# Two more columns in the first of the three products of every input chunk

## The chip, the cores and the metric

The kernel runs on one core of a Trainium2 chip, in one launch. The metric is the device time of that core in microseconds. TensorE is called PE in the profile, its weight loads PEld, VectorE DVE, ScalarE ACT, GpSimd POOL; SyncE (SP) issues the weight stream's DMAs.

## What is computed

The reference is two transformer blocks in float32 over one sequence of 256 tokens with 1024 features. The first holds SwiGLU FFNs, an even mixer (banded and stick-breaking attention), an odd mixer (dilated attention) and two cross attentions; the second holds FFNs and two mixers of differential attention beside a chunked mLSTM. Of its time nearly all goes into dense products of this kind:

```
def swiglu_ffn(x, w_gu, w_down):
    gate, up = jnp.split(x @ w_gu, 2, axis=-1)
    return (jax.nn.silu(gate) * up) @ w_down
```

The sequence is short, so every weight is used once, for 256 tokens.

## The kernel before

Activations are kept feature-major: 8 chunks of 128 features by T = 256 tokens. A float32 product is made out of three float32r products. Each operand is split into a high part (hi, rounded to float32r) and the remainder (lo), and hi by hi, hi by lo and lo by hi are summed in PSUM. The input's two parts lie next to each other per chunk, in `a_two` and `b_two`, [P, C, 2, T]; `a_hi`, `a_lo`, `b_hi`, `b_lo` are views of them.

The weights come as a stream of 829 tiles of 128 x 1024 float32, in the order of use. SP loads each into one of RAW = 4 buffers (`raw`), ACT casts it to `w_hi` (L1072), DVE takes the remainder to `w_lo` (L1508), both rings of RING = 6. PE waits for both parts of a tile (`wait_split`) before its first product.

All matmuls go through the helper `mm` (L462). There are these uses of a weight tile on PE:

- `w_tile` (L468): one output tile of 128 features by 256 tokens, 8 chunks of three products with the weights standing in the array and the tokens moving. It fills columns 0 to 255 of a PSUM bank of 512. FFN gate and up tiles go through it, and so do the projections of the mixers (through `w_next`).
- `three` (L490), `first_three` (L610 in `ffn`) and `tail_part` (L966): the same three products per chunk, but with three tiles taken chunk by chunk as the input comes ready, or a tile in parts.
- `down` in `ffn`: one input chunk into all 8 output chunks, which are two to a bank (`acc(c)`), so both halves of those banks are in use.
- `v_half` (L529): the weights move and the activations stand; two blocks of 128 tokens share a bank, both halves in use.

There are 14 stages in a fixed order, 8 of them FFNs (`STAGES`). An FFN has 22 gate/up pairs and 22 down tiles; after the first few, a `Fori` of 9 turns does two pairs and two down tiles a turn. In it PE runs gate, up and then the down tile of two pairs before. DVE and ACT read the gate and up banks (`gate_up_of`, two pairs of banks in turn), and make the product that `down` needs.

The order of PE's work is the order in which the code above is written. PE waits on semaphores for the weight split, for its banks to be read, and for its inputs.

Of the kernel before, what the change touches and what calls it, by code (L numbers as in the profile page):

```python
# [25 lines left out]
ALU = mybir.AluOpType  # L26
# [5 lines left out]
T = 256  # L32
C = D // P
# [6 lines left out]
RAW = 4  # L40
RING = 6
AHEAD = 4
FFN_TILES = 3 * FJ
C_PATTERNS = ((128, 1), (512, 4), (2048, 16))

# [98 lines left out]
def build(nc, stream_d, x_d, mem_d, vec_d, con_d, biasa_d, biasc_d, heads_d, out_d, stages=STAGES):  # L144
    total = sum(TILES[s] for s, _ in stages)
    with ExitStack() as ctx:
# [8 lines left out]
        a_two = sb("a", [P, C, 2, T], F32R)  # L155
# [46 lines left out]

        def gate_up_of(j, after_mixer):

            return bank[4 + 2 * (j % 2)][:, 0:T], bank[2 if j == 0 and after_mixer else 5 + 2 * (j % 2)][:, 0:T]

        ones = con[:, CON["ones"]:CON["ones"] + P]
        halves = con[:, CON["halves"]:CON["halves"] + 32]
# [236 lines left out]
        def _(pe):  # L445
            t = Tally()
# [10 lines left out]
            act_of = {"a": (a_hi, a_lo), "b": (b_hi, b_lo)}  # L457
            fresh = {}
            rescaled = [False]

            def mm(out, lhsT, rhs, start, stop, shared=False):
                return nc.tensor.matmul(out, lhsT, rhs, start=start, stop=stop, skip_group_check=shared)  # L462
# [5 lines left out]
            def w_tile(n, slot, out, hi, lo, ready=None):  # L468

                wait_split(n)  # L470
                for c in range(C):
                    if ready:
                        ready(c)
                    wh, wl = w_hi[:, slot, c * P:(c + 1) * P], w_lo[:, slot, c * P:(c + 1) * P]
                    mm(out, wh, hi[:, c, :], c == 0, False)
                    mm(out, wh, lo[:, c, :], False, False)
                    last = mm(out, wl, hi[:, c, :], False, c == C - 1)
                return last.then_inc(tile_mm, 1)

            def w_bank(read_by, count):  # L480
# [9 lines left out]
            def three(buf, tiles, where):  # L490

                k, n = turn[0] % 2, at[0]
                outs = [bank[i] for i in where or (W_BANKS[k], W_BANKS[1 - k], T_BANK)]
                hi, lo = act_of[buf]
                ready = fresh.pop(buf)
                for i in range(3):
                    wait_split(n + i)
                    evac_of[tiles[i]] = t.next(w_evac)
                if where is None:
                    turn[0] += 2  # L500
                    last_read[k], last_read[1 - k] = (w_evac, evac_of[tiles[0]]), (w_evac, evac_of[tiles[1]])
                for c in range(C):
                    ready(c)
                    for i in range(3):
                        slot = (n + i) % RING
                        wh, wl = w_hi[:, slot, c * P:(c + 1) * P], w_lo[:, slot, c * P:(c + 1) * P]
                        mm(outs[i][:, 0:T], wh, hi[:, c, :], c == 0, False)
                        mm(outs[i][:, 0:T], wh, lo[:, c, :], False, False)
                        last = mm(outs[i][:, 0:T], wl, hi[:, c, :], False, c == C - 1)
                        if c == C - 1:  # L510
                            last.then_inc(tile_mm, 1)
                at[0] += 3

            def w_next(buf, read_by, where=None):
                if where is None:
                    out = w_bank(read_by, 1)
                else:
                    out = bank[where]
                    t.next(read_by)
                w_tile(at[0], at[0] % RING, out[:, 0:T], *act_of[buf], fresh.pop(buf, None))  # L520
                at[0] += 1

            def v_half(buf, half):
# [81 lines left out]
            def ffn(k, after_mixer):  # L605
                base = k * FJ
                n0 = at[0]
                ready = each(norm_lo)

                def first_three():  # L610

                    outs = [*gate_up_of(0, after_mixer), gate_up_of(1, after_mixer)[0]]
                    for i in range(3):
                        wait_split(n0 + i)
                    for c in range(C):
                        ready(c)
                        for i in range(3):
                            slot = (n0 + i) % RING
                            wh, wl = w_hi[:, slot, c * P:(c + 1) * P], w_lo[:, slot, c * P:(c + 1) * P]
                            mm(outs[i], wh, hi[:, c, :], c == 0, False, True)  # L620
                            mm(outs[i], wh, lo[:, c, :], False, False, True)
                            last = mm(outs[i], wl, hi[:, c, :], False, c == C - 1, True)
                            if c == C - 1:
                                last.then_inc(tile_mm, 1)

                def gate_up(n, slot, j, J):
                    for part, freed in ((0, gate_read), (1, up_read)):
                        pe.wait_ge(freed, J - 1)
                        w_tile(n + part, (slot + part) % RING, gate_up_of(j, False)[part], hi, lo)

                def down(n, slot, jj, J, first=False, final=False):


                    wait_split(n)
                    pe.wait_ge(hlo_done, J + 1)
                    for c in range(C):
                        out = acc(c)
                        wh, wl = w_hi[:, slot, c * P:(c + 1) * P], w_lo[:, slot, c * P:(c + 1) * P]
                        mm(out, wh, h[0][:, jj, :], first and c % 2 == 0, False, True)
                        mm(out, wh, h[1][:, jj, :], False, False, True)  # L640
                        last = mm(out, wl, h[0][:, jj, :], False, final, True)
                        if final and c % 2 and c < C - 1:
                            last.then_inc(acc_done, 1)
                    last.then_inc(tile_mm, 1)

                (hi, lo), h = act_of["a"], act_of["b"]
                s0 = n0 % RING
                first_three()
                if not rescaled[0]:
                    sum_squares(FFN_STAT)  # L650
                w_tile(n0 + 3, (s0 + 3) % RING, gate_up_of(1, False)[1], hi, lo, sums_at_half(FFN_STAT))
                gate_up(n0 + 4, (s0 + 4) % RING, 2, base + 2)
                pe.wait_ge(root_ready, t.so_far(root_ready))
                down(n0 + 6, s0, 0, base, first=True)
                gate_up(n0 + 7, (s0 + 1) % RING, 3, base + 3)
                down(n0 + 9, (s0 + 3) % RING, 1, base + 1)
                with pe.Fori(0, (FJ - 4) // 2) as i:
                    for u in range(2):
                        n, slot, J = i * 6 + (n0 + 10 + 3 * u), (s0 + 10 + 3 * u) % RING, i * 2 + (base + 4 + u)
                        gate_up(n, slot, 4 + u, J)  # L660
                        down(n + 2, (slot + 2) % RING, u, J - 2)
                for j in (FJ - 2, FJ - 1):
                    n = n0 + FFN_TILES - FJ + j
                    down(n, n % RING, j % 2, base + j, final=j == FJ - 1)
                at[0] += FFN_TILES
                if k >= 4:
                    keep_going(1)
                    sum_of_parts()
                    keep_going(7 if k < 7 else 0)
                t.next(x_ready, C)  # L670
# [294 lines left out]
            def tail_part(tile, hi, lo, c0, c1):  # L965
# [6 lines left out]
                out, slot = tail_out[tile]  # L972
                for c in range(c0, c1):
                    wh, wl = w_hi[:, slot, c * P:(c + 1) * P], w_lo[:, slot, c * P:(c + 1) * P]
                    mm(out[:, 0:T], wh, hi[:, c, :], c == 0, False)
                    mm(out[:, 0:T], wh, lo[:, c, :], False, False)
                    last = mm(out[:, 0:T], wl, hi[:, c, :], False, c == C - 1)
                if c1 == C:
# [511 lines left out]
        def _(dve):  # L1490
# [144 lines left out]
            def ffn(k, following, after_mixer):  # L1635
# [2 lines left out]

                def gate_scale(j, n):
                    dve.wait_ge(tile_mm, n + 1)  # L1640
                    nc.vector.tensor_tensor(sil[:, j % 2, :], gate_up_of(j, after_mixer)[0], r, ALU.mult)\  # L1641
                        .then_inc(gate_read, 1)

                def up_scale(j, n):
                    dve.wait_ge(tile_mm, n + 1)
                    nc.vector.tensor_tensor(hmid[:, j % 2, :], gate_up_of(j, after_mixer)[1], r, ALU.mult)\  # L1646
                        .then_inc(up_read, 1)

                def raw_copy(out, source, n, signal):
# [27 lines left out]
                    h_low(u, J)  # L1677

                split_to(n0 + 5)
                raw_copy(sil[:, 0, :], gate_up_of(0, after_mixer)[0], n0, gate_read)  # L1680
                raw_copy(hmid[:, 0, :], gate_up_of(0, after_mixer)[1], n0 + 1, up_read)
                raw_copy(sil[:, 1, :], gate_up_of(1, after_mixer)[0], n0 + 2, gate_read)
                if rescaled[0]:
                    split_to(n0 + 6)
                factors(r, True)
# [690 lines left out]
```

## Time and profile before

| | us |
|---|---|
| median of 3 runs | 2601.88 |
| lowest and highest | 2599.9, 2601.97 |
| span of the profiled execution | 2597.9 |
| PE busy in it | 2562.5 |
| DVE busy | 1787.7 |
| ACT busy | 1389.7 |

The profiled execution is known by its span, from first to last instruction; the median lies 4.0 us above it. PE is busy nearly always, but products are pipelined: one takes some 276 ns from start to end, and the next starts after less than half of that. Its rate is read from starts, or from how many products start in a window, not from its busy share.

### The profile page before, as it was taken

The numbers are of one execution on the slowest core, as the hardware profiler recorded it, in microseconds if no ns is written. First come the engines' busy times: TensorE is split into PE (matmuls) and PEld (weight loads), VectorE is DVE, ScalarE is ACT, GpSimd is POOL, SyncE is SP. The second block draws the span as 40 slices with busy tenths as digits, with TensorE's granted clock in tenths as the row PEclk, the third lists the DMA queues.
The fourth block names the chain that finished last, engine by engine and source line by source line (L and its number), as shares of the span: only waits on it lengthen the run. The fifth ranks groups of instructions, "written<-read, shape, count | busy, mean of one in ns | idle before, by whom it ended". The sixth has DMA issues, their size and how long they took to land.

```text
span 2597.9 us, 56642 instructions
## 1 busy us (share of the span) xinstructions
PE 2562.5 (99%) x21484; PEld 2481.9 (96%) x21484; DVE 1787.7 (69%) x2852; ACT 1389.7 (53%) x2228; POOL 190.8 (7%) x265
## 2 busy tenths in 40 slices
PE   8999999999999999999999999999999999999998
PEld 8998899999998899999999998999999999989998
DVE  7667586667667586767667657776676686677765
ACT  5456556445445755545445555654454465555543
POOL 1001001000000201000000260000000005300000
PEclk9999999999999999999999999999999999999999
DMA  7654245665554354665664543555555545335563
GB/s 272 210 194 138 85 143 181 226 208 188 193 192 158 104 166 142 202 191 176 208 194 158 182 148 105 167 167 193 191 166 188 186 158 173 130 114 179 178 193 114
DMA packets 122830, 445.87 MB, mean 172 GB/s; under 512 B 13688, under 2 KB 14712, under 8 KB 122688
## 3 DMA queue, kind: packets, MB, share of 16 engines
q1 hardware_dynamic: 120816, 436.79, 51.4%
q0 software_dynamic: 1872, 7.11, 0.8%
q8 instruction: 99, 1.62, 0.3%
q14 instruction: 43, 0.35, 0.0%
HBM read 442.79 MB, written 1.05 MB: 171 GB/s over the span
## 4 chain that ended last, share of the span: by engine, by line
PE 93%; DVE 4%; ACT 1%; DMA 1%; issue 0%; SPq 0%; POOL 0%; DVEq 0%; ACTq 0%; POOLq 0%
PE bank L462 92%; DVE w_lo L1508 1%; PE bank L830 1%; DVE x L1623 1%; DVE z L1619 1%; DVE a L1535 0%; DVE score L1559 0%; DVE rstd_x L1527 0%; DMA x<-in_x_dram 0%; DMA heads<-in_heads_dram 0%; ACT score L1304 0%; ACT w_hi L1072 0%; ACT a L1093 0%; DVE rt L1806 0%; DVE rstd_m L1574 0%
## 5 line engine op out<-in xcount | busy, mean ns | idle before, releaser
L462 PE MATMUL bank<-a,w_hi 128*128 128x256 f32 x7472 | 1304.5, 279 | 4.5 <-DVE a L1535 2.7
L1508 DVE TENSOR_TENSOR w_lo<-raw,w_hi 128x1024 fp32r<-128x1024 f32 x829 | 1012.2, 1225 | 201.6 <-ACT w_hi L1072 199.8
L462 PEld LDWEIGHTS bank<-a,w_hi 128*128 128x128 f32 x7472 | 1132.0, 188 | 18.5 <-issue 12.9
L462 PE MATMUL bank<-a,w_lo 128*128 128x256 f32 x3736 | 1035.6, 277 | 0.0
L1072 ACT CAST w_hi<-raw 128x1024 fp32r<-128x1024 f32 x829 | 842.7, 1044 | 51.9 <-DMA raw<-in_stream_dram 48.7
L462 PE MATMUL bank<-b,w_hi 128*128 128x256 f32 x4800 | 839.5, 278 | 2.8 <-DVE w_lo L1508 2.8
L462 PEld LDWEIGHTS bank<-b,w_hi 128*128 128x128 f32 x4800 | 727.4, 188 | 10.6 <-issue 5.7
L462 PEld LDWEIGHTS bank<-a,w_lo 128*128 128x128 f32 x3736 | 702.7, 188 | 0.0
L462 PE MATMUL bank<-b,w_lo 128*128 128x256 f32 x2400 | 664.8, 277 | 0.0
L462 PEld LDWEIGHTS bank<-b,w_lo 128*128 128x128 f32 x2400 | 450.9, 188 | 0.0
L1132 ACT CAST b<-hmid 128x256 fp32r<-128x256 f32 x132 | 53.7, 407 | 393.9 <-PE bank L462 383.5
L1646 DVE TENSOR_TENSOR hmid<-bank,rstd_x 128x256 f32<-128x256 f32 x168 | 71.2, 424 | 161.3 <-PE bank L462 161.2
L1128 ACT ACTIVATE sil<-sil 128x256 f32<-128x256 f32 x176 | 73.5, 418 | 149.9 <-DVE sil L1641 142.9
L1508 DVE TENSOR_TENSOR b<-hmid,b 128x256 fp32r<-128x256 f32 x132 | 56.1, 425 | 126.9 <-ACT b L1132 126.6
L462 PE MATMUL bank<-w_hi,a 128*128 128x256 f32 x736 | 130.7, 281 | 0.0
L2185 POOL TENSOR_SCALAR score<-score,rr 128x128 f32<-128x128 f32 (+1 forms) x96 | 44.5, 479 | 1100.9 <-DVE rr L1874 804.2
L462 PEld LDWEIGHTS bank<-w_hi,a 128*128 128x128 f32 x736 | 111.9, 188 | 3.4 <-issue 2.5
L1745 DVE TENSOR_TENSOR z<-bank,rstd_x 128x256 f32<-128x256 f32 x121 | 51.1, 422 | 77.2 <-PE bank L462 76.4
L462 PE MATMUL bank<-w_lo,a 128*128 128x256 f32 x368 | 102.2, 278 | 0.0
L1132 ACT CAST a<-hmid 128x256 fp32r<-128x256 f32 x44 | 17.9, 407 | 136.0 <-PE bank L462 132.7
L1660 DVE TENSOR_TENSOR hmid<-sil,hmid 128x256 f32<-128x256 f32 x176 | 74.8, 425 | 6.8 <-ACT sil L1128 1.1
L1641 DVE TENSOR_TENSOR sil<-bank,rstd_x 128x256 f32<-128x256 f32 x160 | 67.8, 424 | 13.0 <-PE bank L462 2.8
(191 smaller groups left out, 1924.3 us busy)
## 6 DMA issues: line engine op xcount, KB each, us to landing
raw<-in_stream_dram SPq DMA_DIRECT2D x829, 512.0 KB, 3.7
z<-in_biasc_dram POOLq DMA_DIRECT2D x6, 512.0 KB, 4.6
z<-in_biasa_dram POOLq DMA_DIRECT2D x3, 512.0 KB, 5.0
x<-in_x_dram SPq DMA_DIRECT2D x2, 512.0 KB, 8.1
v<-in_mem_dram POOLq DMA_DIRECT2D x2, 512.0 KB, 5.7
out_dram<-x SPq DMA_DIRECT2D x8, 128.0 KB, 1.9
con<-in_con_dram POOLq DMA_DIRECT2D x1, 848.0 KB, 6.4
vec<-in_vec_dram POOLq DMA_DIRECT2D x1, 417.0 KB, 5.6
```

The source lines that it names most:

```text
L462: return nc.tensor.matmul(out, lhsT, rhs, start=start, stop=stop, skip_group_check=shared)
L830: last = nc.tensor.transpose(out[:, col:col + P], p[:, src:src + P], ident)
L1072: nc.scalar.copy(w_hi[:, slot, :], raw[:, raw_slot, :]).then_inc(hi_split, 1)
L1128: nc.scalar.activation(sil[:, jj, :], sil[:, jj, :], ACT.Silu).then_inc(silu_done, 1)
L1132: nc.scalar.copy(high_of["b"][:, jj, :], hmid[:, jj, :]).then_inc(hhi_done, 1)
L1508: return nc.vector.tensor_tensor(out, a, hi.bitcast(F32), ALU.subtract)
L1619: nc.vector.tensor_tensor(temp[:, c, :], x[:, c, :], rt[:, 0, 0:T], ALU.mult).then_inc(dve_step, 1)
L1641: nc.vector.tensor_tensor(sil[:, j % 2, :], gate_up_of(j, after_mixer)[0], r, ALU.mult)\
L1646: nc.vector.tensor_tensor(hmid[:, j % 2, :], gate_up_of(j, after_mixer)[1], r, ALU.mult)\
L1660: nc.vector.tensor_tensor(hmid[:, jj, :], sil[:, jj, :], hmid[:, jj, :], ALU.mult)\
L1745: nc.vector.tensor_tensor(z[:, tile, :], out[:, 0:T], rstd[norm][:, :], ALU.mult).then_inc(w_evac, 1)
L2185: last = nc.gpsimd.tensor_scalar(p, p, rr[:, k, b:b + 1], 1.0, ALU.mult, ALU.mult)
```

## The change

A function `first_product` takes the place of the first `mm` (hi by hi) in `w_tile`, `three`, `first_three` and `tail_part`. It reads T + EXTRA = 258 columns in place of 256 and writes 258 columns of the bank. The two more columns read are the first two of the same chunk's lo part, which lies right behind hi (`both_of`); they land in columns 256 and 257 of the bank, in the half that these tiles leave unused. The other two products of the chunk stay at 256 columns. `down` and `v_half` are not changed. The readers of the banks take columns 0 to 255 as before; `gate_up_of` now gives whole banks, and its readers slice them.

```
+EXTRA = 2
...
-            return bank[4 + 2 * (j % 2)][:, 0:T], bank[2 if j == 0 and after_mixer else 5 + 2 * (j % 2)][:, 0:T]
+            return bank[4 + 2 * (j % 2)], bank[2 if j == 0 and after_mixer else 5 + 2 * (j % 2)]
...
+            both_of = dict((id(hi), two[:, :, :, :].rearrange("p c h t -> p c (h t)")) for hi, two in ((a_hi, a_two), (b_hi, b_two)))
+
+            def first_product(out, wh, hi, c, shared=False):
+
+                n = T + EXTRA
+                mm(out[:, 0:n], wh, both_of[id(hi)][:, c, 0:n], c == 0, False, shared)
...
-                    mm(out, wh, hi[:, c, :], c == 0, False)
-                    mm(out, wh, lo[:, c, :], False, False)
-                    last = mm(out, wl, hi[:, c, :], False, c == C - 1)
+                    first_product(out, wh, hi, c)
+                    mm(out[:, 0:T], wh, lo[:, c, :], False, False)
+                    last = mm(out[:, 0:T], wl, hi[:, c, :], False, c == C - 1)
```

The same three lines change in `three`, `first_three` and `tail_part`. No instruction moves on any engine. On PE, in the FFN loop, this is the end of an up tile (input `a`), the step to the next weight tile, and the beginning of a down tile (input `b`). Before:

```order
L462 MATMUL bank<-a,w_hi 128x256 x2
L462 MATMUL bank<-a,w_lo 128x256
L465 REGISTER_ALU
L462 MATMUL bank<-b,w_hi 128x256 x2
L462 MATMUL bank<-b,w_lo 128x256
```

And with the change, at the same place:

```order
L469 MATMUL bank<-a,w_hi 128x258
L469 MATMUL bank<-a,w_hi 128x256
L469 MATMUL bank<-a,w_lo 128x256
L472 REGISTER_ALU
L469 MATMUL bank<-b,w_hi 128x256 x2
L469 MATMUL bank<-b,w_lo 128x256
```

The first of the two w_hi products of an up tile's chunk has 258 columns; those of the down tile are as they were.

## Rows read from the trace of the kernel before

**Rows 1.** The page: span, and part 1, busy time, share of the span, instructions

```profile
span 2597.9 us, 56642 instructions
...
PE 2562.5 (99%) x21484; PEld 2481.9 (96%) x21484; DVE 1787.7 (69%) x2852; ACT 1389.7 (53%) x2228; POOL 190.8 (7%) x265
```

**Rows 2.** The page's part 4, the chain that ended last, by line

```profile
PE bank L462 92%; DVE w_lo L1508 1%; PE bank L830 1%; DVE x L1623 1%; DVE z L1619 1%; DVE a L1535 0%; DVE score L1559 0%; DVE rstd_x L1527 0%; DMA x<-in_x_dram 0%; DMA heads<-in_heads_dram 0%; ACT score L1304 0%; ACT w_hi L1072 0%; ACT a L1093 0%; DVE rt L1806 0%; DVE rstd_m L1574 0%
```

**Rows 3.** The view of waits, PE: who waited for whom, us, times, longest

```profile
PE bank L462 <- ACT w_hi L1072: 5.2, 1, 5.2
```

**Rows 4.** Groups of PE, shapes apart: w_lo products, standing weights | busy, mean ns

```profile
L462 PE MATMUL bank<-a,w_lo 128*128 128x256 f32 x3736 | 1035.6, 277 | 0.0
...
L462 PE MATMUL bank<-b,w_lo 128*128 128x256 f32 x2400 | 664.8, 277 | 0.0
```

**Rows 5.** The chain in order of time, 1728 to 2090 us: start, us, what

```profile
1728.58 163.89 PE bank L462 x1442
...
1915.88 170.27 PE bank L462 x1442
```

**Rows 6.** Windows, L462 on PE: length, busy us (x products), clock, DMA share, GB/s

```profile
1732.00:1892.00 160.00, 160.00 (x1414) 1.00 0.62 203
1920.00:2080.00 160.00, 160.00 (x1361) 1.00 0.60 195
```

**Rows 7.** The timeline of PE, a fast stretch, then a slow one: start, us

```profile
1820.14 0.39 PE L462 MATMUL bank<-b,w_hi 128*128 128x256 f32 x2
1820.37 0.28 PE L462 MATMUL bank<-b,w_lo 128*128 128x256 f32 x1
1820.48 0.39 PE L462 MATMUL bank<-b,w_hi 128*128 128x256 f32 x2
...
2010.30 0.40 PE L462 MATMUL bank<-b,w_hi 128*128 128x256 f32 x2
...
2010.65 0.40 PE L462 MATMUL bank<-b,w_hi 128*128 128x256 f32 x2
```

**Rows 8.** The timeline of PE, the start of the same two stages

```profile
1728.58 0.48 PE L462 MATMUL bank<-b,w_hi 128*128 128x256 f32 x2 [1.01 <-DVE w_lo L1508]
...
1729.02 0.39 PE L462 MATMUL bank<-b,w_hi 128*128 128x256 f32 x2
1729.25 0.28 PE L462 MATMUL bank<-b,w_lo 128*128 128x256 f32 x1
...
1915.88 0.47 PE L462 MATMUL bank<-b,w_hi 128*128 128x256 f32 x2 [0.76 <-DVE w_lo L1508]
...
1916.31 0.40 PE L462 MATMUL bank<-b,w_hi 128*128 128x256 f32 x2
1916.55 0.28 PE L462 MATMUL bank<-b,w_lo 128*128 128x256 f32 x1
```

**Rows 9.** The timeline of PEld, weight loads, in the fast and the slow stretch

```profile
1820.37 0.30 PEld L462 LDWEIGHTS bank<-b,w_hi 128*128 128x128 f32 x2
...
2010.18 0.31 PEld L462 LDWEIGHTS bank<-b,w_hi 128*128 128x128 f32 x2
```

**Rows 10.** L830's products: timeline, and the line's own, min/median/max ns

```profile
1539.87 0.49 PE L830 MATMUL bank<-con,score 128*128 128x128 f32 x3
...
L830 PE MATMUL bank<-con,score x152: 270/273/330, 238.2 to 2244.2; 128*128 128x128 f32 x152
```

**Rows 11.** Windows as in rows 6: the first and the last slow stretch

```profile
192.50:200.50 8.00, 8.00 (x70) 1.00 0.20 61
...
2409.00:2413.00 4.00, 4.00 (x36) 1.00 0.01 4
```

**Rows 12.** Windows as in rows 6: weights moving, a slow and a fast stretch

```profile
1500.00:1515.00 15.00, 15.00 (x130) 1.00 0.53 173
...
2142.00:2162.00 20.00, 20.00 (x179) 1.00 0.63 208
```

**Rows 13.** The page's part 5: DVE's half of the weight split | busy, mean ns

```profile
L1508 DVE TENSOR_TENSOR w_lo<-raw,w_hi 128x1024 fp32r<-128x1024 f32 x829 | 1012.2, 1225 | 201.6 <-ACT w_hi L1072 199.8
```

More of the change, by code:

```diff
@@ L506, in three @@
                         wh, wl = w_hi[:, slot, c * P:(c + 1) * P], w_lo[:, slot, c * P:(c + 1) * P]
-                        mm(outs[i][:, 0:T], wh, hi[:, c, :], c == 0, False)
+                        first_product(outs[i], wh, hi, c)
                         mm(outs[i][:, 0:T], wh, lo[:, c, :], False, False)
@@ L519, in w_next @@
                     t.next(read_by)
-                w_tile(at[0], at[0] % RING, out[:, 0:T], *act_of[buf], fresh.pop(buf, None))
+                w_tile(at[0], at[0] % RING, out, *act_of[buf], fresh.pop(buf, None))
                 at[0] += 1
@@ L619, in first_three @@
                             wh, wl = w_hi[:, slot, c * P:(c + 1) * P], w_lo[:, slot, c * P:(c + 1) * P]
-                            mm(outs[i], wh, hi[:, c, :], c == 0, False, True)
-                            mm(outs[i], wh, lo[:, c, :], False, False, True)
-                            last = mm(outs[i], wl, hi[:, c, :], False, c == C - 1, True)
+                            first_product(outs[i], wh, hi, c, True)
+                            mm(outs[i][:, 0:T], wh, lo[:, c, :], False, False, True)
+                            last = mm(outs[i][:, 0:T], wl, hi[:, c, :], False, c == C - 1, True)
                             if c == C - 1:
@@ L974, in tail_part @@
                     wh, wl = w_hi[:, slot, c * P:(c + 1) * P], w_lo[:, slot, c * P:(c + 1) * P]
-                    mm(out[:, 0:T], wh, hi[:, c, :], c == 0, False)
+                    first_product(out, wh, hi, c)
                     mm(out[:, 0:T], wh, lo[:, c, :], False, False)
@@ L1640, in gate_scale @@
                     dve.wait_ge(tile_mm, n + 1)
[L1641 removed]
+                    nc.vector.tensor_tensor(sil[:, j % 2, :], gate_up_of(j, after_mixer)[0][:, 0:T], r, ALU.mult)\
                         .then_inc(gate_read, 1)
@@ L1645, in up_scale @@
                     dve.wait_ge(tile_mm, n + 1)
-                    nc.vector.tensor_tensor(hmid[:, j % 2, :], gate_up_of(j, after_mixer)[1], r, ALU.mult)\
+                    nc.vector.tensor_tensor(hmid[:, j % 2, :], gate_up_of(j, after_mixer)[1][:, 0:T], r, ALU.mult)\
                         .then_inc(up_read, 1)
@@ L1679, in ffn @@
                 split_to(n0 + 5)
-                raw_copy(sil[:, 0, :], gate_up_of(0, after_mixer)[0], n0, gate_read)
-                raw_copy(hmid[:, 0, :], gate_up_of(0, after_mixer)[1], n0 + 1, up_read)
-                raw_copy(sil[:, 1, :], gate_up_of(1, after_mixer)[0], n0 + 2, gate_read)
+                raw_copy(sil[:, 0, :], gate_up_of(0, after_mixer)[0][:, 0:T], n0, gate_read)
+                raw_copy(hmid[:, 0, :], gate_up_of(0, after_mixer)[1][:, 0:T], n0 + 1, up_read)
+                raw_copy(sil[:, 1, :], gate_up_of(1, after_mixer)[0][:, 0:T], n0 + 2, gate_read)
                 if rescaled[0]:
```

## The prediction

> **What bounds the kernel now.** I read first the page's busy times, then the chain that ended last, then the PE groups, and last the starts of single products. PE is busy for 99% of the span [rows 1], and matmuls of the helper line L462 alone hold 92% of the chain [rows 2]. PE's waits are small: the longest entry is 5.2 us, once, for the first weight split [rows 3]. TensorE's granted clock reads full, 1.00, in every stretch used below, which is its upper level of 2.4 GHz. So the time is a count of products times their spacing, and whatever changes the spacing changes the end one for one.
>
> The count: where the weights stand in the array, a chunk takes three products (w_hi by the input's high part, w_hi by its low part, w_lo by its high part). The w_lo ones are 3736 + 2400 = 6136 [rows 4], so there are 6136 such triples, 18,408 products. The triples of the FFN's down products, which the change leaves alone, are 22 tiles x 8 chunks x 8 FFN stages = 1408. The change touches the other 4728.
>
> The spacing is not one number. The chain holds the steady part of two FFN stages in a row, the same 1442 products each: 163.89 us in the one, 170.27 us in the other, 6.38 us apart [rows 5]. The windows say the same: 1414 products start in 160 us of the first stage and 1361 in 160 us of the second, which is 113.2 ns and 117.6 ns each at the same clock, and DMA share is no higher in the slow one (0.60 against 0.62) [rows 6]. The single starts show it as a rhythm: in the fast stretch one triple follows the other by 0.34 us (1820.14, 1820.48), in the slow one by 0.35 (2010.30, 2010.65) [rows 7]. By the starts over a whole stretch I take 113.3 and 117.8 ns, 4.4 ns apart (6.38 us / 1442 gives the same).
>
> Which rhythm a stretch has is settled within the first three or so products after PE has stood still, and then kept: from the first product to the fourth the two stages take 0.44 and 0.43 us, from the fourth to the sixth 0.23 and 0.24 us, and they stay apart for 1442 products [rows 8]. Nothing waits in between. So the slow rhythm is not work of its own; it is a state that PE's own streams fall into.
>
> **What the change does, part by part.**
>
> 1. *Two more columns in 4728 products.* TensorE takes 256 columns at 2.4 GHz in 106.7 ns, and 258 in 107.5, so 0.83 ns more each: 4728 x 0.83 = 3.9 us if all of it lay in the spacing. I take 0 for it. In the fast rhythm a product starts every 113.3 ns, which leaves 6.6 ns behind its last column, and the next weight load begins only as a product begins (1820.37 in both views), the next product 0.11 us after that (1820.48) [rows 7, 9]: the load, not the stream of columns, seems to release the next product. The nearest rows of another kind are 128-column fp32 products of L830, each with its own load: three of them take 0.49 us with 0.273 us for one, so some 0.11 us each [rows 10]. They stay at or under the fast spacing. The bounds for this part are therefore 0 and +3.9 us in the fast rhythm; a product that is pushed past some further slot is rival C.
>
> The row shows 113.3 ns. The Trainium skill (TensorE: Matmul & The Clock Gate, Back-to-back issue gap) puts the warm gap of one product at its columns over 2.4 GHz plus 2.5 ns, which would be 109.2 ns before and 110.0 after, and by that rule the change costs 3.9 us if the stream sets the spacing. The same page (LDWEIGHTS) puts a weight load at its columns over 1.2 GHz, 106.7 ns for 128, untouched here, so if the load sets the spacing the columns are free. No trace row gives 109.2 for these products, so neither rule describes the spacing whole.
>
> 2. *What becomes of the slow rhythm.* This is the term of the sum. With weights standing, I find 26 stretches of nine or more slow gaps, 3288 products in all: the first at 192.4 us with 70, the last at 2408.8 us with 37, the longest the FFN stage at 1916 us with 1438; three others have 226 and one 261 [rows 6, 11]. They cost 3288 x 4.44 ns = 14.6 us. A rhythm that repeats exactly triple after triple (353.3 ns, against 340.0) needs the three products to be alike. With the change each triple has one product whose columns end 0.83 ns later, in a rhythm whose own excess is only 4.4 ns a product, so the point at which the streams meet moves with each triple. I expect that the slow rhythm is not held by such triples and runs on until it falls into the fast one, which has the slack of part 1. The bounds: nothing gained (0), and all of it (-14.6 us). I take nearly all, -14 us, with some 0.5 us for the 26 settlings.
>
> 3. *What is not touched.* The down products keep three alike, but they come 24 at a time behind 48 changed ones, and a rhythm once found is kept. The products in which the weights move (v halves, 1488) are not changed; 934 of them are slow in 23 stretches, as in the window at 1500 us with 130 in 15 us where another of the same kind has 179 in 20 us [rows 12]. They cost 4.1 us; I leave that as it is, since they start behind short waits of their own. DVE, ACT, POOL and the DMA issues have the same instructions. The slices of the bank they read are the same 256 columns; the two extra columns land where nobody reads. The faster PE asks for weights no sooner than it does in the other stages, where DVE's half of the split (1225 ns a tile) [rows 13] fits in a tile of 24 x 113.3 = 2720 ns. So nothing new comes late.
>
> The sum, against the profiled execution: span 2597.9 - 14 = 2584; the median of the three runs is 4.0 us above that span, so 2601.9 - 14 = 2588 us.
>
> **Rivals.**
>
> A. The forecast: the slow rhythm goes with weights standing. 2587 if all goes, 2598 if only the shorter stretches do, since the FFN stage at 1916 us holds 6.4 of the 14.6 us. Chance 0.42. For: two rhythms, one program, chosen at a restart. Against: I infer from starts how the streams meet; no row shows it.
>
> B. Nothing to measure: the weight load sets the spacing in both rhythms and hides the columns in both, or they cost up to their 3.9 us. 2598 to 2606. Chance 0.22. For: the load begins with the product before it in both rhythms, and its row reads 0.30 and 0.31 us for two [rows 9].
>
> C. Slower, and the one on the other side: the fast rhythm is the delicate one. If the first product's 258 columns end past the point at which the next product or its load takes its turn, the next must wait for another turn. The price is what the slow rhythm shows, since there is no other: 353.3 - 340.0 = 13.3 ns for a triple at full price, half of it (6.7 ns) if the other two products catch up. Over 4728 triples that is 31 us at half, so 2633; at full price for all triples that are fast now, (18,408 - 3288) / 3 = 5040, 67 us, 2669. It decides at 113.3 ns: if a product's natural time is within 0.83 ns of it, C holds. The L830 rows stand against, with 0.11 us. Chance 0.19.
>
> D. The choice is drawn afresh: both rhythms survive, but the first products after each restart fall otherwise. One of eight FFN stages is slow now, while of all stretches with a rhythm of their own (a dozen gaps or more) 49 in 151 are, by the starts. A draw at that rate would give two or three slow stages, 6.4 us each: 2608 to 2615. Chance 0.17 (of which 0.02 for a lucky draw that comes out faster).
>
> **How the numbers follow.** Likeliest is A, 2588 us. A's own range is 2580 to 2598. A range for 8 in 10 takes in A, B, D and the lower half of C: 2579 to 2636. About 0.2% (5 us) is what a measurement of this kernel can tell from no change, so faster is A and the lucky part of D, 0.44; same is B and a little of D, 0.22; slower is C and the rest of D, 0.34.
>
> **What the profile of the changed kernel would show.** Part 1: in a steady FFN stage 1414 products in 160 us as now; 1400 or fewer would say that the columns are in the spacing. Part 2: the steady part of every FFN stage at 164 us for 1442 products in the chain, the one at 1916 us too; if one still reads 170, the slow rhythm is held by uneven triples and A is wrong. Part 3: the windows of v halves as now, some slow. C would show as triples of 0.35 us in nearly every stage, D as other stages slow than now. The prediction fails if the two rhythms turn on something that I can't see in these rows, such as where operands lie in SBUF, which the change leaves alone.

## The result and the profile after

| | before | after |
|---|---|---|
| median, us | 2601.88 | 2674.23 |
| runs | 3, 2599.9 to 2601.97 | 3, 2673.84 to 2677.43 |
| span of the profiled execution, us | 2597.9 | 2671.9 |

The changed kernel is slower: 1.0288 of the time before, 95% interval 1.0255 to 1.032. The forecast was 2588 us, range 2579 to 2636.

The page after, span and part 1, to read beside [rows 1]:

```profile
span 2671.9 us, 56642 instructions
...
PE 2639.9 (99%) x21484; PEld 2559.4 (96%) x21484; DVE 1789.2 (67%) x2852; ACT 1388.6 (52%) x2228; POOL 189.1 (7%) x265
```

The products are as many as before, 21484, and PE is busy for the same share. DVE and ACT have not changed. The time is again in the spacing of the products. From the chain in order of time of the changed kernel, the steady part of the same two FFN stages as in [rows 5], and above them the longest piece:

```profile
412.64 443.45 PE bank L469 x3728
...
1780.89 170.05 PE bank L469 x1442
...
1974.34 170.06 PE bank L469 x1442
```

And the longest piece in the kernel before:

```profile
403.69 428.23 PE bank L462 x3728
```

The two stages, 163.89 and 170.27 us before, now take 170.05 and 170.06: the fast one has lost 6.2 us, the slow one has gained 0.2. The longest piece has gone from 428.23 to 443.45 us for the same 3728 products. Windows inside the two stages, as in [rows 6] (length, busy us, products, clock, DMA share, GB/s):

```profile
1783.00:1943.00 160.00, 160.00 (x1361) 1.00 0.59 195
1977.00:2137.00 160.00, 160.00 (x1360) 1.00 0.59 195
```

1361 and 1360 products in 160 us, where the fast stage had 1414, with the clock at 1.00. Taken alone, this reads as if the slow rhythm (353.3 ns for the three products of a chunk, a triple) were everywhere. The timeline says otherwise. Five starts from the changed kernel, the end of a down tile (256 columns throughout) and the start of a gate tile:

```profile
1850.94 0.39 PE L469 MATMUL bank<-b,w_hi 128*128 128x256 f32 x2
...
1851.29 0.39 PE L469 MATMUL bank<-b,w_hi 128*128 128x256 f32 x2
...
1851.62 0.40 PE L469 MATMUL bank<-a,w_hi 128*128 128x258 f32 x2
...
1851.98 0.40 PE L469 MATMUL bank<-a,w_hi 128*128 128x258 f32 x2
...
1852.34 0.40 PE L469 MATMUL bank<-a,w_hi 128*128 128x258 f32 x2
```

The down triple takes 1851.29 - 1850.94 = 0.35 us here at 10 ns a step (340 to 341 ns by the starts), so the down tiles run in the fast rhythm. The triples with a 258-column product take 0.36 us, 1851.62 to 1851.98 to 1852.34. By all starts in the trace, counting every triple that another follows within 400 ns, 4054 of 4475 changed triples take 359 to 361 ns (mean of all 359.6), and 1219 of 1400 down triples take 339 to 341. The means of other runs below are taken in the same way. So there is a third rhythm, of 360 ns a triple, that the profile before did not show: slower than the slow one's 353.3. Within a changed triple the products follow at 118.9, 118.4 and 122.3 ns on average, so all three are late and not just the one behind the long product.

The sum of it: both traces have the same 21484 products in the same order, so each spacing can be set against its own from before. Where it is under 150 ns in both, those of the changed triples have grown by 76.5 us in all (13,979 spacings), those of the v halves by 2.0, and those of the down tiles have shrunk by 1.3. That is 77 us; the spans are 74.0 apart, so the longer spacings, with the waits in them, have given some 3 us back.

### The profile page after: what moved, and what is told of

It is laid out like the page before. It is cut to its first block, busy times and chain, and to the rows that moved or that the text cites. A ratio compares the mean times of both kernels' runs of the same rounds, so it can differ in the third digit from the quotient of the medians.

```text
span 2671.9 us, 56642 instructions
## 1 busy us (share of the span) xinstructions
PE 2639.9 (99%) x21484; PEld 2559.4 (96%) x21484; DVE 1789.2 (67%) x2852; ACT 1388.6 (52%) x2228; POOL 189.1 (7%) x265
## 4 chain that ended last, share of the span: by engine, by line
PE 94%; DVE 4%; ACT 1%; issue 0%; DMA 0%; SPq 0%; DVEq 0%; ACTq 0%
PE bank L469 93%; DVE w_lo L1515 1%; PE bank L837 1%; DVE x L1630 1%; DVE z L1626 1%; DVE a L1542 0%; DVE score L1566 0%; DVE rstd_x L1534 0%; DMA raw<-in_stream_dram 0%; ACT a L1100 0%; ACT w_hi L1079 0%; DVE rt L1813 0%; DVE rstd_m L1581 0%; ACT score L1311 0%; DVE z L1611 0%
## 5 line engine op out<-in xcount | busy, mean ns | idle before, releaser
L469 PE MATMUL bank<-a,w_hi 128*128 128x256 f32 (+1 forms) x7472 | 1357.5, 283 | 3.0 <-DVE a L1542 2.2
L469 PEld LDWEIGHTS bank<-a,w_hi 128*128 128x128 f32 x7472 | 1157.2, 188 | 16.8 <-issue 12.4
L469 PE MATMUL bank<-a,w_lo 128*128 128x256 f32 x3736 | 1061.5, 284 | 0.0
L469 PE MATMUL bank<-b,w_hi 128*128 128x258 f32 (+1 forms) x4800 | 859.5, 281 | 1.7 <-DVE w_lo L1515 1.7
L469 PEld LDWEIGHTS bank<-b,w_hi 128*128 128x128 f32 x4800 | 737.4, 188 | 9.5 <-issue 4.6
L469 PEld LDWEIGHTS bank<-a,w_lo 128*128 128x128 f32 x3736 | 710.5, 190 | 0.0
L469 PE MATMUL bank<-b,w_lo 128*128 128x256 f32 x2400 | 674.6, 281 | 0.0
```

## The experiments

All runs but those of the inputs' place are written from the changed kernel, and times are compared with the kernel before on the same chip, whose medians in the four sets were 2604.6, 2602.9, 2605.3 and 2603.1 us.

### Shorter, longer by 16 columns, and a pair that makes up for itself

A shorter product, with the first back at 256 columns:

```
-EXTRA = 2
+EXTRA = 0
...
-                    mm(out[:, 0:T], wh, lo[:, c, :], False, False)
+                    mm(out[:, 0:T - 2], wh, lo[:, c, 0:T - 2], False, False)
```

> The first product of every chunk is back at 256 columns; the second one (hi by lo) has 254, so the last two tokens miss that small term. Measured so far: a changed triple takes 360 ns in place of 340 or 353. Theory 1 (alignment: the fast rhythm of 113.3 ns needs products whose lengths are all alike or keep step with a clock of the chip; any odd length, longer or shorter, throws the next product off step): the triples stay near 355 to 360 ns though they do less work, 2655 to 2680 us. Theory 2 (length: only a product that is too long misses its turn, and 258 columns is too long): a shorter product costs nothing, 2580 to 2605 us.

Measured: 2650.9 us, ratio 1.0183 (1.0139 to 1.0226). Changed triples take 353.1 ns on average, though each has less work than before. It's not the two columns of work that cost, and not only that a product is too long for its turn: a product two columns too short costs 46 us, where one two columns too long costs 70 to 72.

The FFN stages of this run are not all alike:

```profile
1764.43 168.04 PE bank L469 x1442
...
2467.48 170.27 PE bank L469 x1442
```

In the one at 1764 us the changed triples take 344 to 357 ns and most down triples 340. The one at 2467 us is in the slow rhythm throughout: all 304 triples with a 254-column product that were counted take 352 to 355 ns. So uneven triples can hold the slow rhythm.

Sixteen more columns:

```
-EXTRA = 2
+EXTRA = 16
```

> EXTRA = 16: the first product of every chunk has 272 columns, 14 more than in the changed kernel, or 6.7 ns more work in each of 4728 products. Theory 1 (alignment): start times in the trace of before keep to a step of 6.67 ns, which is 16 columns at 2.4 GHz, so 272 columns stay in step: a triple takes 340 + 6.7 = 347 ns at most, 2601.9 + 31 = 2633 us or less (2619 if the slow stretches go too), faster than with 258 columns. Theory 2 (length): longer is worse, 360 ns or more a triple, 2674 us or more.

Measured: 2675.9 us, ratio 1.0279 (1.0235 to 1.0323), 358.7 ns a triple. Theory 1 in the form in which I had it, that any multiple of 16 columns stays in step, is wrong. The product behind the 272-column one comes 124.3 ns later and the next two at 117.5 and 116.8: near the slow rhythm's spacing, with 6.7 ns more for the 16 columns behind the long one.

The first product two longer, the second two shorter:

```
-                    mm(out[:, 0:T], wh, lo[:, c, :], False, False)
+                    mm(out[:, 0:T - 2], wh, lo[:, c, 0:T - 2], False, False)
```

> First product 258 columns, second 254 (the last two tokens miss the hi by lo term), third 256: the sum of a triple is again 768. Theory 1 (alignment): two products in the triple start off step, but the third is back on it, so the triple should cost less than 360 ns, some 345 to 355, 2620 to 2655 us. Theory 2 (length of the long product alone): as the changed kernel, 2670 to 2676 us.

Measured: 2630.0 us, ratio 1.0099 (1.0069 to 1.013), most triples 346 or 347 ns. Two odd products that cancel cost less than either alone. So the number of odd products is not what counts. That the products have to come back to a step fits this run, but 272 columns, 16 more, did not behave so.

### All three alike

```
+            def second_product(out, wh, hi, c, shared=False):
+                n = T + (EXTRA if c < C - 1 else 0)
+                mm(out[:, 0:n], wh, flat_of[id(hi)][:, (2 * c + 1) * T:(2 * c + 1) * T + n], False, False, shared)
...
-                    last = mm(out[:, 0:T], wl, hi[:, c, :], False, c == C - 1)
+                    last = third_product(out, wl, hi, c)
```

The second product reads on into the next chunk's high part, the third into its own chunk's low part.

> 258 columns in all three products of a chunk in the tiles that go through w_tile with all their input ready (the FFN's gate and up tiles and most of the mixers'; the last chunk's second product stays at 256, and the other uses have 258 in the first and third). The prediction held that a rhythm needs three products that are alike. If likeness is what counts, these triples take 340 to 343 ns, 2600 to 2635 us. If the length itself has to fit (256 columns do, 258 don't), they take 353 ns or more, 2650 to 2690 us.

Measured: 2716.3 us, ratio 1.043 (1.0397 to 1.0463). A triple of three 258-column products takes 365.5 ns on average, 121.8 ns a product, and the single ones are spread from 360 to 374, with no length that most of them have. So three like products need not give a rhythm that repeats, and they are slower here than the changed kernel's uneven ones. The down tiles, fast behind the changed kernel's triples, are slow behind these (353.4 ns).

The same with EXTRA = 16:

> 272 columns in all three products where all input is ready (elsewhere in the first and third), as the run with 258 columns in all three. If the fast rhythm needs alike products in step with 16 columns, these triples take 340 + 20 = 360 ns, about as long as the changed kernel's 360, 2670 to 2690 us. If 272 columns have only the slow rhythm, 117.8 + 6.7 = 124.4 ns a product and 373 ns a triple, some 2730 us or more.

Measured: 2738.0 us in one run; three 272-column products take 370.6 ns, 123.5 each, near the 124.4 of the slow rhythm with 6.7 ns more. For 272 columns no fast rhythm shows: none of these triples takes less than 369 ns, where 340 + 20 = 360 would be the fast one.

### What sets the pace: fewer and more columns

Half of the second product left out, 128 columns in place of 256:

```
-EXTRA = 2
+EXTRA = 0
...
-                    mm(out[:, 0:T], wh, lo[:, c, :], False, False)
+                    mm(out[:, 0:128], wh, lo[:, c, 0:128], False, False)
```

> Leaves half of the hi by lo product out: first and third product of a chunk have 256 columns, the second has 128, in the same 4728 chunks. The second's columns take 53 ns, half of a weight load's 128 columns would still have to come. Theory 1 (the load sets the fast spacing of 113.3 ns, as the prediction had it): the product after the short one still comes some 110 to 118 ns later, a changed triple takes 340 to 360 ns, 2590 to 2680 us. Theory 2 (the stream of columns sets it): it comes well under 100 ns later, a triple takes 290 to 300 ns, some 2370 to 2420 us.

Measured: 2630.4 us in one run. Most changed triples take 343 to 350 ns, none less than 341, with half of the second product's columns gone. The starts of the products (a row with x2 has the first and second):

```profile
1799.98 0.34 PE L469 MATMUL bank<-a,w_hi 128*128 128x256 f32 x2
1800.15 0.33 PE L469 MATMUL bank<-a,w_lo 128*128 128x256 f32 x1
1800.32 0.34 PE L469 MATMUL bank<-a,w_hi 128*128 128x256 f32 x2
```

And of the weight loads in the same triples:

```profile
1800.10 0.19 PEld L469 LDWEIGHTS bank<-a,w_lo 128*128 128x128 f32 x1
1800.21 0.30 PEld L469 LDWEIGHTS bank<-a,w_hi 128*128 128x128 f32 x2
1800.44 0.19 PEld L469 LDWEIGHTS bank<-a,w_lo 128*128 128x128 f32 x1
```

The product behind the short one starts early, 0.17 us after the first (1799.98 to 1800.15), and the next one waits, another 0.17. The loads show why. They begin at 1800.10 and 1800.21 (a pair of w_hi), and the next of w_lo at 1800.44: three steps, 0.34 us from w_lo to w_lo. They go on at a little over 0.11 us each, though the products have a sixth less to stream. So the columns don't set the floor, and it is not a fixed distance from product to product either, since the one behind the short product starts 60 ns after it. What is left, and goes once with each product, is the load of the weights, as the prediction had it; that is by exclusion, for no run changed the loads.

All three products at 240 columns (chunk 0's first product stays at 256):

```
-EXTRA = 2
+EXTRA = -16
...
-                n = T + EXTRA
+                n = T + (EXTRA if c else 0)
...
-                    mm(out[:, 0:T], wh, lo[:, c, :], False, False)
-                    last = mm(out[:, 0:T], wl, hi[:, c, :], False, c == C - 1)
+                    mm(out[:, 0:240], wh, lo[:, c, 0:240], False, False)
+                    last = mm(out[:, 0:240], wl, hi[:, c, 0:240], False, c == C - 1)
```

> All three products of a chunk have 240 columns (the last 16 tokens get only the first chunk's first product; 16 columns are 6.7 ns, the step on which start times lie). Theory 1 (load sets the fast spacing): 340 ns a triple at best, as before, 2590 to 2680 us. Theory 2 (stream sets it, and the fast rhythm holds for lengths that are a multiple of 16 columns): 320 ns a triple, 2602 - 4728 x 20 ns = 2507 us. Theory 3 (stream sets it, but 240 columns have only the slow rhythm, 117.8 - 6.7 = 111.1 ns a product): 333 ns, some 2570 us.

Measured: 2601.3 us in one run. The timeline:

```profile
1800.24 0.39 PE L469 MATMUL bank<-a,w_hi 128*128 128x240 f32 x2
1800.46 0.28 PE L469 MATMUL bank<-a,w_lo 128*128 128x240 f32 x1
1800.58 0.39 PE L469 MATMUL bank<-a,w_hi 128*128 128x240 f32 x2
```

0.34 us a triple, about as the fast rhythm with 256 columns, with 16 columns fewer in each product. By all starts the mean is 338.6 ns, where columns alone would have taken 20 ns off; the shortest take 332, so 340 is not quite the floor. (The down tiles, left at 256, are slow in this run, 353 ns, so the time is not below the kernel before.) The Trainium skill (TensorE: Matmul & The Clock Gate, LDWEIGHTS) has a load's time go by its own columns, 106.7 ns for 128, whatever the product streams; that is 6.6 ns under the 113.3 measured between products, and no run here changed a load's columns.

512 columns in the first product:

```
-EXTRA = 2
+EXTRA = 256
```

> EXTRA = 256: the first product has 512 columns, so the stream of columns and not the weight load must set its spacing. With 272 columns the product after the long one came 124.3 ns later, 6.5 ns more than the slow rhythm's 117.8, which is the time of 16 columns. If off the fast rhythm the columns' stream sets the spacing, this one comes 117.8 + 106.7 = 224.5 ns later, a changed triple takes some 460 ns and the kernel some 3150 us. If a weight load set it, the first product would hide part of its added columns, 213 to 218 ns, 3110 us or less.

Measured: 3181.1 us in one run. The product behind the 512-column one comes 230.0 ns later on average (226 to 233), nearer to 224.5 than to 218: with long products the stream of columns sets the spacing, with 17 ns on top of its 213.3.

So the runs fit two chains: loads at 111 to 113 ns each, and the stream of columns, 106.7 ns for 256 of them and something on top that depends on how they meet. At 256 columns the two are nearly equal. That the rhythms come from this is argued, and not shown.

### What the fast rhythm keeps step with

The kernel before, all products at 256 columns, with the inputs a and b moved in SBUF by 8 bytes:

```
-        sb("gap_b", [P, 64])
-        b_two = sb("b", [P, C, 2, T], F32R)
+        sb("gap_b", [P, 56])
+        b_two = sb("b", [P, C * 2 * T + 8], F32R)[:, 2:2 + C * 2 * T].rearrange("p (c h t) -> p c h t", c=C, h=2)
```

and the same for `a_two`; everything else stays where it was.

> The kernel before with the input arrays a and b moved by 8 bytes (2 columns) in SBUF, all products at 256 columns. Open is what the fast rhythm keeps step with. If it is where a product's columns begin or end in SBUF (258 columns end 8 bytes further), the fast rhythm is lost in all products with a or b moving, whose triples take 353 ns or more: 2665 us or more. If it is the count of columns alone, nothing changes: 2592 to 2616 us as before.

Measured: 2703.4 us, ratio 1.0391 (1.0343 to 1.044). The timeline of an FFN stage:

```profile
1850.42 0.40 PE L462 MATMUL bank<-b,w_hi 128*128 128x256 f32 x2
...
1850.78 0.40 PE L462 MATMUL bank<-b,w_hi 128*128 128x256 f32 x2
```

0.36 us a triple, exactly 120.00 ns a product over every steady FFN stage. The same 360 ns as a triple of the changed kernel, with no product longer than 256. And the three like products don't follow evenly: in most triples they come at 116, 119 and 125 ns. With 8 in place of 2 (32 bytes):

> As the run with 8 bytes, with 32 bytes in place of 8. If addresses matter in pieces of 32 bytes, this one keeps the fast rhythm where the 8-byte one loses it, 2592 to 2616 us. If the distance between inputs and weights matters, both lose it. If only the count of columns matters, both are as before.

Measured: 2672.9 us, ratio 1.0274 (1.0226 to 1.0323). The steady FFN stage of 1442 products in the chain of the two runs, 8 bytes first, then 32:

```profile
1798.51 173.47 PE bank L462 x1442
```

```profile
1780.75 171.07 PE bank L462 x1442
```

173.47 and 171.07 us against 163.89 or 170.27 in [rows 5]. Both lose the fast rhythm; 32 bytes do not bring it back. So the place of the inputs in SBUF counts. In the v halves the same inputs stand in the array and the weights move, and there it counts too: with 8 bytes 270 of 449 such triples take 350 ns, a length that none has in the kernel before, where they take 340 or 353. So it is not the place of the moving operand alone. Whether an operand's own place decides, or its distance from the other one, these runs don't tell. The Trainium skill says that loading the next weights "doesn't steal SBUF read bandwidth from the running matmul" (TensorE: Matmul & The Clock Gate, Step-by-step: what each phase is for). By that, the two reads of PE don't get in each other's way. The 6.7 ns a product that 8 bytes cost here would fit reads that do meet, but that is my reading, and not shown: no run here tells it from a cost of the place by itself.

### Odd products as a kick

One long product at the head of each tile, none elsewhere:

```
-                n = T + EXTRA
+                n = T + (EXTRA if c == 0 else 0)
```

> 258 columns only in the first product of a tile (chunk 0), 591 products in place of 4728. In the changed kernel's trace the first unchanged triple after changed ones takes 345 ns and all that follow 340, so an isolated long product should cost 15 + 5 = 20 ns, 591 x 20 = 11.8 us. If it throws the slow rhythm out as well, the 14.6 us of the slow stretches go: 2599 us. If the slow rhythm survives it: 2614 us. If the fast rhythm doesn't come back after one long product, some 2650 to 2670 us.

Measured: 2598.6 us, ratio 0.9974 (0.9956 to 0.9992). The timeline over one kick:

```profile
1800.48 0.39 PE L469 MATMUL bank<-b,w_hi 128*128 128x256 f32 x2
...
1800.82 0.40 PE L469 MATMUL bank<-a,w_hi 128*128 128x258 f32 x2
...
1801.17 0.39 PE L469 MATMUL bank<-a,w_hi 128*128 128x256 f32 x2
...
1801.52 0.39 PE L469 MATMUL bank<-a,w_hi 128*128 128x256 f32 x2
...
1801.86 0.39 PE L469 MATMUL bank<-a,w_hi 128*128 128x256 f32 x2
```

The triple with the long product takes 0.35 us (1800.82 to 1801.17; 355 ns by the starts), the next 0.35 (345), and then it is 0.34 again: 15 + 5 = 20 ns, and the fast rhythm is back by itself. Repeated in every triple, as in the changed kernel, some 20 ns are paid each time and the rhythm never comes back. Two of the FFN stages in its chain:

```profile
1732.31 164.74 PE bank L469 x1442
...
2421.61 164.74 PE bank L469 x1442
```

Both are fast, at the price of their kicks (164.7 for 163.9 us), and so are the other six: 113.9 ns a product. Of 26 kicks with three slow triples right before them, 24 were followed by the fast rhythm. The runs spread from 2596.7 to 2602.3 us, those of the kernel before beside them from 2597.1 to 2616.2.

With fewer kicks, a product of 258 columns once per FFN stage, behind its last wait (`w_tile` passes `extra` on for chunk 0 alone, and all other first products have 256):

```
-                gate_up(n0 + 7, (s0 + 1) % RING, 3, base + 3)
+                gate_up(n0 + 7, (s0 + 1) % RING, 3, base + 3, EXTRA)
```

> One product of 258 columns per FFN stage, in the first gate tile after the last wait of the stage's start; all else has 256 columns. In the run with 258 columns at the head of every tile, 24 of 25 such products that met the slow rhythm were followed by the fast one, and 3 of 424 that met the fast one by the slow. If one odd product is enough to leave the slow rhythm and the fast one then holds by itself, every FFN stage's steady 1442 products take 164 us, and the time lies at the lower end of what the kernel before gives (its runs spread from 2597 to 2616): 2595 to 2600 us, with little spread. If it takes a kick in every tile to stay fast, some runs will still have slow FFN stages, 2602 us and above as before.

Measured: 2596.0 us (2591.4 to 2605.3), ratio 0.9972 (0.9956 to 0.9988). But in its profile two of eight stages are slow, kick or no kick:

```profile
1726.05 163.91 PE bank L469 x1442
...
1913.37 170.28 PE bank L469 x1442
...
2419.84 170.28 PE bank L469 x1442
```

With kicks at the mixers' tiles as well:

```
-                w_tile(at[0], at[0] % RING, out, *act_of[buf], fresh.pop(buf, None))
+                w_tile(at[0], at[0] % RING, out, *act_of[buf], fresh.pop(buf, None), EXTRA)
```

> As the run with one 258-column product per FFN stage, and one also at chunk 0 of every tile of the mixers and cross attentions that goes through w_next (some 210 tiles), where short waits start PE anew. Each costs 20 ns, 4 us in all. In the first profile the mixers' tiles held some 1850 slow products with weights standing, 8.2 us. If kicks clear those: 2590 to 2596 us. If the kick costs as much as it brings there: 2595 to 2600 us, as with the FFN kicks alone.

Measured: 2597.7 us (2592.7 to 2609.1), ratio 0.9984 (0.9967 to 1.0), one FFN stage slow. With seven kicks per FFN stage ahead of its loop (the chunks of the gate and of the up tile whose first product is long) and the mixers' kicks:

```
-                gate_up(n0 + 4, (s0 + 4) % RING, 2, base + 2)
+                gate_up(n0 + 4, (s0 + 4) % RING, 2, base + 2, ((0,), (0, 3)))
...
-                gate_up(n0 + 7, (s0 + 1) % RING, 3, base + 3)
+                gate_up(n0 + 7, (s0 + 1) % RING, 3, base + 3, ((0, 5), (0, 1)))
```

> 258 columns in seven first products per FFN stage, in its four gate and up tiles between the last wait and the loop (chunk 0 of each, and chunks 3, 5 and 1), and at chunk 0 of the mixers' tiles that go through w_next; none in the FFN loops. Some 270 long products, 5.4 us. One kick per FFN stage left two of eight stages slow; several at different distances should leave none, 6.4 us each. With one kick and with the mixers' kicks the medians were 2596.0 and 2597.7: 2590 to 2595 us if the kicks work, 2596 to 2602 if whether a stage is fast stays a matter of chance.

Measured: 2598.7 us, ratio 0.9974 (0.9963 to 0.9985), again one stage of eight slow, at 117.8 ns. One of its twelve runs took 7455.09 us; the record gives no cause, the ratio leaves it out, and the median of the other eleven is 2598.1. One kick per turn of the FFN loop:

```
-                        gate_up(n, slot, 4 + u, J)
+                        gate_up(n, slot, 4 + u, J, ((0,), ()) if u == 0 else ((), ()))
```

> 258 columns in one first product per turn of the FFN loop (chunk 0 of one gate tile in each turn, 72 products in all), nowhere else. Seven long products before the loop left one FFN stage in eight slow; one in every tile left none slow, at 20 ns each. If repetition is what clears the slow rhythm, every FFN stage runs its 1439 products at 113.4 to 113.6 ns each, for 1.4 us in all: 2592 to 2598 us. If the fixed distance of a turn lets the slow rhythm survive, one or more stages stay at 117.8 ns and the median at 2600 us or more.

Measured: 2596.5 us (2592.7 to 2609.1), ratio 0.9978 (0.9956 to 0.9999), and in its profile two of eight stages slow:

```profile
1731.08 170.33 PE bank L469 x1442
...
2424.55 170.33 PE bank L469 x1442
```

In these two stages 18 kicks met the slow rhythm, and none cleared it. In the stage at 20 us one did. First a kick that failed, then the one that worked, each with the two triples behind it:

```profile
1742.46 0.40 PE L469 MATMUL bank<-a,w_hi 128*128 128x258 f32 x2
...
1742.82 0.40 PE L469 MATMUL bank<-a,w_hi 128*128 128x256 f32 x2
...
1743.18 0.40 PE L469 MATMUL bank<-a,w_hi 128*128 128x256 f32 x2
```

```profile
39.94 0.40 PE L469 MATMUL bank<-a,w_hi 128*128 128x258 f32 x2
...
40.29 0.40 PE L469 MATMUL bank<-a,w_hi 128*128 128x256 f32 x2
...
40.64 0.39 PE L469 MATMUL bank<-a,w_hi 128*128 128x256 f32 x2
```

By the starts the failed one takes 360 ns and the next triple 354, the other 357 and 346.

The last, with the mixers' kicks added:

> As the run with one long product per loop turn, and one at chunk 0 of the mixers' tiles that go through w_next (some 212). The mixers' slow stretches cost 5.5 us of the 8.2 that a first profile showed with such products, which cost 4.2 us themselves: about the same as without them, 2590 to 2597 us, or 4 us more if they bring nothing.

Measured: 2602.2 us, ratio 1.0 (0.998 to 1.0021), one FFN stage slow.

A kick does not clear the slow rhythm for sure, but it is not chance either. The fast rhythm's starts lie on one step of 6.67 ns. Against that step, the three products of a slow triple stand about 1.7, 3.3 and 5.8 ns late, in one of three orders, and a stage keeps its order. Over the profiles of these six runs 133 kicks had three slow triples right before them. Where the kicked product, the first of the triple, stood at 1.7 or 3.3, the fast rhythm followed each time (38 and 55); where it stood at 5.8, it never followed (40). This was read from the traces afterwards; a kick on the second or third product was not run.

Only the run with one in every tile had all eight stages fast, in the one profile that there is of it. Its two FFN stages that began slow stood at 3.3; the order that a kick doesn't clear came up twice, outside the FFN stages, and was not cleared there either. Of these six variants three lie 0.26 to 0.28% below the kernel before with intervals that leave out 1 and a fourth 0.22%, just so; the other two can't be told from it. How many stages start slow would account for a run at 2592 or at 2609 us, but each variant has one profile only. The variant with one kick per tile has the narrowest spread, for 12 us of kicks.

## Why the prediction was wrong

**What bounds the kernel** was right: the spacing of products decides, one for one, and 74 us of span came from spacing alone. The counts (4728 changed triples, 1408 of down products) hold. The two rhythms are there, and the down tiles keep the fast one.

**Part 1, "I take 0 for it"**, is the step that failed. Its inner claim, that not the columns set the 113.3 ns, was right: 240 columns run hardly faster (112.9 ns), and a triple with a 128-column product no faster. That it is the weight load is left by exclusion. What doesn't follow is that columns within the 6.6 ns of slack are free. The bounds of 0 and +3.9 us were bounds on work. The true cost was another: 15 + 5 ns for a single long product in the fast rhythm, and 359.6 - 340.0 = 19.6 ns a triple when each has one, 4728 x 19.6 = 93 us against a kernel that is all fast. The reasoning took two chains of nearly equal length and asked which was longer; a product with two columns fewer also costs, so length is not the question.

**Part 2, that uneven triples don't hold the slow rhythm**, was half right and wrong in what it stood for. The slow rhythm did go from those triples; what came was not the fast one but a third, slower. The premise that a rhythm wants three like products fell with the changed kernel itself, whose uneven triples repeat at 360 ns, and with the stage of the 254-column run whose uneven triples hold the slow rhythm. Nor are three like products enough for it: 258 columns in all three take 365.5 ns and don't repeat. I had taken the fast rhythm for the natural state, to which things fall back. From the fast rhythm a single long product does fall back to it, within two triples, when the next products are undisturbed; with one odd product in each triple they never are. From the slow rhythm it depends on where in the step the long product stands.

**Part 3**: down tiles as said, and faster than before by 0.9 ns a triple (1.3 us in 1408); the v halves nearly all slow now (6 of 449 triples at 340 ns, before 150 at 339 to 341), +2 us.

**Rival C** had it: the fast rhythm is the delicate one, full price 2669 us, measured 2674. Its price was built from the slow rhythm, "since there is no other", on all triples that were fast: 13.3 ns on 5040. In truth it's 19.6 ns on 4728, and nothing on the down tiles, which comes out near by chance. I gave it 0.19 and let its half price bound the range, on the word of the L830 rows [rows 10]. Those are fp32 products whose load takes 141 ns in the trace, against 188 for these; they were no measure of how the two streams of float32r meet. Rival D, a new draw at each restart, is not what happened: all eight FFN stages slowed alike, at 117.6 or 117.7 ns a product.

The prediction's last sentence named what was not seen: where operands lie in SBUF. That place does change the rhythm, by the run with 8 bytes, but no run shows that it is why 258 columns do. It should have weighed more: the gaps `gap_a`, `gap_b`, `gap_w` in the code hold no data and only set places.

**What stays open.** Why two columns or 8 bytes cost what they do, whether and where the two streams meet, and what puts a stage into one order of the slow rhythm or another. The start times of the fast rhythm lie on one step of 6.67 ns across all of the execution, and the lengths 340, 346.7, 353.3 and 360 ns are whole numbers of such steps. What the step belongs to, no run has shown.

## What to carry to other kernels

Where a product's columns and the next weights' load take nearly the same time, the spacing need not be the longer of the two, and it can change by 4 to 6% with two columns more or less or with 8 bytes in an operand's place. Read it from starts over a long stretch, look for more than one rhythm in the same code, and measure an edit to lengths or places before trusting any slack in it. That something else sets the floor does not make a product of odd length free.

## What was not expected of the hardware

- Products with 240 columns run at 112.9 ns and with 256 at 113.3, and a 128-column one saves nothing: the weight loads beside them, of 128 columns, follow each other at 0.11 us at best.
- Inputs moved by 8 bytes: exactly 120.00 ns a product in place of 113.3; by 32 bytes, 118.3.
- Triples of 256-column products at a granted clock of 1.00 took 340 or 353.3 ns in one and the same execution, and 360 with the inputs 8 bytes away. The choice between the first two at a restart moves an FFN stage by 6.4 us, and would account for much of the spread of the kernel before, 2589 to 2616 us over the runs here; one profile of it was taken.
- The slow rhythm has three forms that differ by which product stands where in a step of 6.67 ns; in 133 of 133 cases the form told whether a 258-column product would end it.
- 258 columns in all three products are slower, 121.8 ns, than the 0.8 ns more than the slow rhythm that their columns would add.
